# Index scores in pairs inside three input strips, the search from later strips on, and the layers written out

## What is computed

```python
dots = jnp.einsum('bthd,bsd->bths', qi.astype(jnp.float32), ki_all.astype(jnp.float32))
score = jnp.einsum('bth,bths->bts', wi.astype(jnp.float32), jax.nn.relu(dots))
allowed = (k_pos[None, :] // CHUNK) <= (q_pos[:, None] // CHUNK)
score = jnp.where(allowed[None], score, -jnp.inf)
top_val, top_idx = lax.top_k(score, topk)
...
logits = jnp.einsum('btngd,btknd->btngk', qg, kg).astype(jnp.float32) * (HEAD_DIM ** -0.5)
logits = jnp.where(valid[:, :, None, None, :], logits, -jnp.inf)
p = jax.nn.softmax(logits, axis=-1).astype(vg.dtype)
o = jnp.einsum('btngk,btknd->btngd', p, vg)
```

## Time and profile before

| | us |
|---|---|
| median of three runs (3303.45 to 3306.64) | 3303.59 |
| the profiled execution | 3304.65 |
| its span, first to last instruction | 3302.9 |
| layer 1: index scores between strips K and V | 175.05 to 226.60 |
| layer 1: end of the last count behind AU1 | 407.5 |
| change of layer, PE's first matmul of layer 2's norm | 1693.9 |

### The profile page before, as it was taken

The page is one execution under the profiler, slowest core; times in us unless marked ns, Lnnn a source line. Parts: engine busy times, 40 slices in busy tenths (PEclk is TensorE's granted clock), DMA queues, the critical chain, the costliest instruction groups (busy, mean ns, idle before and its releaser), DMA issues.

```text
span 3302.9 us, 44102 instructions
## 1 busy us (share of the span) xinstructions
PE 2926.2 (89%) x15746; PEld 2505.2 (76%) x15770; DVE 1611.5 (49%) x2488; ACT 1147.8 (35%) x1378; POOL 817.7 (25%) x340
## 2 busy tenths in 40 slices
PE   6699866788899999999979996678898999999996
PEld 6659732237799999999965993223688999999996
DVE  7658667653333232433455776666324414333244
ACT  1335737843321111111142483685324111111113
POOL 0101126711122222222210111763021222322221
PEclk9969978998899999999986997899899999999998
DMA  8202300010122222222211121001012222222222
GB/s 348 83 18 70 128 2 1 1 32 21 51 76 81 65 91 69 83 76 70 77 57 33 55 92 58 0 1 32 13 57 69 79 67 82 66 90 72 67 86 81
DMA packets 70265, 214.71 MB, mean 65 GB/s; under 512 B 17280, under 2 KB 17536, under 8 KB 69120
## 3 DMA queue, kind: packets, MB, share of 16 engines
q1 hardware_dynamic: 67504, 202.71, 18.2%
q10 hardware_dynamic: 2640, 10.49, 0.8%
HBM read 196.76 MB, written 15.87 MB: 64 GB/s over the span
## 4 chain that ended last, share of the span: by engine, by line
issue 50%; PE 30%; POOL 12%; DVE 4%; ACT 2%; DVEq 1%; POOLq 0%; ACTq 0%; DMA 0%
PE ps L823 26%; POOL cy L527 6%; POOL w_lo L501 6%; PE ps L998 1%; PE ps L982 1%; PE ps L1068 1%; ACT notsel L622 0%; PE ps L1047 0%; DVE smax L1424 0%; POOL hp L520 0%; DVE notsel L1305 0%; DVE s_keep L1257 0%; DVE notsel L1302 0%; DVE rank_samp L1297 0%; DVE negmax L1436 0%
## 5 line engine op out<-in xcount | busy, mean ns | idle before, releaser
L501 POOL TENSOR_TENSOR w_lo<-w_raw,w_hi 128x1024 fp32r<-128x1024 f32 x202 | 501.1, 2481 | 2207.4 <-ACT w_hi L582 2207.4
L823 PE MATMUL ps<-h_hi,w_hi 128*128 128x352 f32 x2928 | 646.6, 329 | 64.4 <-DVE h_lo L1126 50.1
L823 PE MATMUL ps<-h_hi,w_lo 128*128 128x352 f32 x2928 | 636.3, 325 | 0.0
L823 PE MATMUL ps<-h_lo,w_hi 128*128 128x352 f32 x2928 | 636.1, 326 | 0.0
L823 PEld LDWEIGHTS ps<-h_hi,w_hi 128*128 128x128 f32 x2928 | 502.8, 191 | 88.3 <-DVE h_lo L1126 61.5
L823 PEld LDWEIGHTS ps<-h_hi,w_lo 128*128 128x128 f32 x2928 | 507.0, 189 | 0.0
L823 PEld LDWEIGHTS ps<-h_lo,w_hi 128*128 128x128 f32 x2928 | 502.8, 190 | 0.0
L582 ACT CAST w_hi<-w_raw 128x1024 fp32r<-128x1024 f32 x202 | 211.2, 1045 | 643.3 <-PE ps L823 404.1
L527 POOL TENSOR_TENSOR cy<-cy,ctmp 128x1086 f32<-128x1086 f32 x120 | 302.3, 2520 | 234.2 <-ACT ctmp L708 224.4
L622 ACT ACTIVATE notsel<-score,s_cand 128x384 bf16<-128x384 f32 (+3 forms) x248 | 297.3, 1200 | 139.2 <-DVE s_cand L1245 139.0
L1528 DVE TENSOR_TENSOR act_f<-silu,ps 128x1056 f32<-128x1056 f32 x44 | 55.2, 1254 | 593.7 <-PE ps L823 593.7
(11 more groups left out here) (222 smaller groups left out, 3389.1 us busy)
## 6 DMA issues: line engine op xcount, KB each, us to landing
w_ada<-in_w_ada SPq DMA_DIRECT2D x96, 512.0 KB, 5.1
w_raw<-in_w_up SPq DMA_DIRECT2D x88, 512.0 KB, 3.4
w_raw<-in_w_in SPq DMA_DIRECT2D x34, 512.0 KB, 3.6
w_ada<-in_w_ada SPq DMA_DIRECT2D x7, 2048.0 KB, 12.2
w_raw<-in_w_down SPq DMA_DIRECT2D x32, 384.0 KB, 3.1
w_ada<-in_w_ada ACTq DMA_DIRECT2D x5, 2048.0 KB, 12.2
w_raw<-in_w_down SPq DMA_DIRECT2D x32, 320.0 KB, 2.9
spill<-stage SPq DMA_DIRECT2D x16, 528.0 KB, 2.6
```

The lines of the kernel that those rows point to most:

```text
L501: nc.gpsimd.tensor_tensor(w_lo[slot][:], w_raw[:], w_hi[slot][:].bitcast(F32), ALU.subtract)\
L823: last = nc.tensor.matmul(ps[:, bank + t, 0:TW], wt[slot][:, kk, :], mv[:, kk, t * TW:(t + 1) * TW], start=(kk == 0 and p == 0), stop=(kk ...
```

## The change

Three things change, and one follows from them.

1. The index scores are computed two heads at a time: heads 2hp and 2hp + 1 lie in the two halves of the partitions, and their contractions go to banks 6 and 7 together. There are 20 pairs in place of 40 steps; a pair has one ReLU over both banks on ACT and two operations on DVE. The pairs no longer stand between strips K and V. They are issued by `beside` behind the contraction blocks 0 to 6 of strips V, Q0 and Q1 (`PAIRS_IN`: 7, 7 and 6). All pairs use the same two banks, so a pair waits for the ReLU of the pair before. The two ReLU buffers are now the two buffers `probs` of the attention.
2. The search starts behind Q1's score pairs; `SEARCH_AFTER` gives one step behind Q1, two behind Q2 and Q3, three behind CA0 to AV1 and AU0, five behind AU1. The sample's index chunks move from V and later to Q2 and later (`SAMPLE_AFTER`), with SP's loads of their keys.
3. On every engine the loop over layers is a Python loop: the program contains both layers, and the values to wait for are constants, except in the inner loops that stay.

What follows: the copy of the sample's queries (`q_samp`) moves from Q3 to CG1, and ACT's copy of CA0 no longer waits for the sample's sums.

```diff
+PAIRS_IN = {4: (0, 7), 5: (7, 14), 6: (14, 20)}
+PAIR_AFTER = (0, 1, 2, 3, 4, 5, 6)
...
-SEARCH_AFTER = {S_V: 2, S_Q0: 2, S_Q1: 2, S_Q2: 2, S_Q3: 2, S_CA0: 3, S_CA1: 3, S_CG0: 3, S_CG1: 3, S_AV0: 3,S_AV1: 3, S_AU0: 2, S_AU1: 1}
+SEARCH_AFTER = {S_Q1: 1, S_Q2: 2, S_Q3: 2, S_CA0: 3, S_CA1: 3, S_CG0: 3, S_CG1: 3, S_AV0: 3, S_AV1: 3, S_AU0: 3, S_AU1: 5}
+SAMPLE_AFTER = S_Q2
...
+        relu = probs
...
-            with pe.Fori(0, DEPTH) as l:
+            for l in range(DEPTH):
                 rms(l, 0)
+
+                def dots(n):
+
+                    _, i, c, w, hp = DOTS[n]
+                    if n >= 1:
+                        pe.wait_ge(relu_ready.sem, relu_ready.at(l, n))
+                    for e in range(2):
+                        r = slice(64 * e, 64 * e + 64)
+                        last = nc.tensor.matmul(ps[:, 6 + e, 0:w], qi[r, hp, i * P:(i + 1) * P], ki[r, c:c + w], start=True, stop=True)
+                    last.then_inc(dots_ready.sem, 1)
...
-                    if j == S_K:
-                        for n in range(N_DOTS):
-                            relu_step(n, 6 + n % 2, DOTS[n][3])
-                    if S_V <= j < S_V + 5:
-                        c = j - S_V
+                    for n in range(*PAIRS_IN.get(j + 1, (0, 0))):
+                        relu_step(n, 2, DOTS[n][3])
+                    if SAMPLE_AFTER <= j < SAMPLE_AFTER + 5:
+                        c = j - SAMPLE_AFTER
...
-                    if j == S_K:
-                        for n, (sn, i, c, w, h) in enumerate(DOTS):
-                            sc = score[:, SC_AT[sn] + c:SC_AT[sn] + c + w]
-                            dve.wait_ge(relu_ready.sem, relu_ready.at(l, n + 1))
+                    for n in range(*PAIRS_IN.get(j + 1, (0, 0))):
+                        sn, i, c, w, hp = DOTS[n]
+                        sc = score[:, SC_AT[sn] + c:SC_AT[sn] + c + w]
+                        dve.wait_ge(relu_ready.sem, relu_ready.at(l, n + 1))
+                        for e in range(2):
+                            h = 2 * hp + e
...
+                    if j == S_Q0:
                         for sn, i in enumerate(SEARCHED):
...
-                    if j == S_K:
-
                         dve.drain()
                         start_search(0, PSRCH)
```

More of the change, by code:

```diff
@@ L168, in build @@
         swapped = place("swapped", Z_O, [P, TOK], F32)
-        relu = [place(f"relu{s}", Z_O + CYB + s * 2048, [P, 512], F32) for s in range(2)]
         wiT = place("wiT", Z_O + CYB, [P, TOK], F32)
@@ L497, in _ @@
         def _(pool):
-            with pool.Fori(0, DEPTH) as l:
+            for l in range(DEPTH):
                 def split_lo(j, slot):
@@ L604, in _ @@
                     nc.scalar.activation(cond_row[:], cond_row[:], ACT.Silu).then_inc(row_ready.sem, 1)
-            with act.Fori(0, DEPTH) as l:
+            for l in range(DEPTH):
                 act.wait_ge(x_fed.sem, x_fed.at(l, 0))
@@ L813, in rms, with strip @@
                 last.then_inc(rms_summed.sem, 1)
-            def strip(l, j, slot, bank, nk, hi, lo, k_ready=None):
+            def strip(l, j, slot, bank, nk, hi, lo, k_ready=None, beside=None):
                 pe.wait_ge(w_ready.sem, w_ready.at(l, j + 1))
@@ L825, in strip @@
                                                     start=(kk == 0 and p == 0), stop=(kk == nk - 1 and p == 2))
-                last.then_inc(w_used.sem, 1)
+                    if kk == nk - 1:
+                        last.then_inc(w_used.sem, 1)
+                    if beside is not None:
+                        beside(kk)
             pe.wait_ge(const_loaded.sem, 32)
@@ L849, in _, with dots_beside @@
                         pe.wait_ge(wi_rows.sem, wi_rows.at(l, 1))
-                    strip(l, j, j % 2, strip_bank(j), KD, h_hi, h_lo, (h_ready, 0) if j == 0 else None)
+                    if j == S_V:
+                        pe.wait_ge(idx_rot.sem, idx_rot.at(l, 3))
+                        pe.wait_ge(ki_twice.sem, ki_twice.at(l, 16))
+                        pe.wait_ge(wi_ready.sem, wi_ready.at(l, 1))
+                    def dots_beside(kk):
+                        first, end = PAIRS_IN[j]
+                        if kk in PAIR_AFTER and first + PAIR_AFTER.index(kk) < end:
+                            dots(first + PAIR_AFTER.index(kk))
+                    strip(l, j, j % 2, strip_bank(j), KD, h_hi, h_lo, (h_ready, 0) if j == 0 else None,
+                          dots_beside if j in PAIRS_IN else None)
                     if j == S_QI1:
@@ L1200, in _ @@
             swap_pairs = [i ^ 1 for i in range(32)]
-            with dve.Fori(0, DEPTH) as l:
+            for l in range(DEPTH):
                 norm(l, 0)
```

56 lines of the change are left out of this document (23 added, 33 removed).

## The result

The changed kernel takes 3274.11 us, the median of four runs (3271.37 to 3275.21), and the kernel before took 3304.36 beside it: a ratio of 0.9906, with a 95% interval of 0.9889 to 0.9923. It is 30 us faster. The forecast was 3274, from 3258 to 3290.

The account below looks back on a forecast made before the run. Bound: PE up to the last score, then the DVE and ACT search chain to the counts' end. Gains 2 x 12.8 + 3.2 + 1 = 29.8 us off 3304.65 give 3274.9, less 1.06 for the median: 3274, range 3258 to 3290.

Parts of the forecast that it names:

- What bounds the stage: Scores and search: PE spends 53.6 us a layer on scores and aftermath, then DVE and ACT set the pace until the counts end.
- The pairs: Twenty score pairs in strips V, Q0 and Q1: 14.1 us of columns plus 4.0 fixed, 18.1; with three strips 53.2.
- the sum by its rule: Total if each of the twenty score pairs pays twice for switching the tiling mode: 3276.
- The waits between pairs: Each pair waits for the previous ReLU: about 0.4 us left for two handovers, just enough; Q1's third ReLU 1.1 us late.
- The search: Last score to end of counts on DVE and ACT: 165.4 us instead of 179.0; counts end 12.8 us earlier per layer.
- The layer change: Between the two layers: writing them out removes the jump back, saving 3.2 us, once.
- Constants: Wait values in both layers become constants instead of computed registers: 1 us gained in all, bounds 0 and 10.
- A: Rival, score pairs: handover too tight, each pair waits half a microsecond for its ReLU, 10 us a layer; 3294, chance 0.08.
- B: Rival, score stage: PE is the bound after all, so 34.4 us a layer come through; 3231, chance 0.07.
- C: Rival, score pairs among strips: PE falls to the lower clock, adding 49.2 us a layer; 3372, chance 0.04.
- D: Rival, behind the counts: they end earlier but the next stage starts no earlier; 3299, chance 0.03.

## Why the prediction was right, point by point

**What bounds the stage.** Right. I had read 53.6 us a layer of PE's time in the stage and its aftermath; AU1's last matmul comes 31.6 us earlier against K's rotation, and only 12 of these reach the end of the counts. Moving steps from late to early strips changed nothing, lengthening the pairs on PE by 14.4 us a layer cost all of it, and hiding one step paid its 4.0. So PE is last up to the last score, the chain of DVE and ACT from there on. The wait of 2 to 3 us that I expected of PE before CA1 is not there; between the weave and AU1's end PE never waits longer than 0.2 us.

**The pairs.** This step was mis-sized. I took 0.2 us beside the columns, from the attention's pair, and a bound of 0.05 more from the earlier trace rows. It is 0.40, so twenty pairs take 21.9 us and not 18.1. The rows that I used held it: in the earlier trace rows the strip's first group behind the sample's contraction (241.35) takes 0.75 us where a group in the stream takes 0.65, and I left that 0.1 out; with it and the issue ahead, those rows give 1.2 for a pair and not 1.1. Whether the attention's pair hides the same 0.1 in the matmuls behind it, its rows do not separate. The Trainium skill (TensorEngine Tiling (Array Packing), Key Properties) says that switching the tiling mode drains TensorE; the run with each pair twice agrees, 0.40 us for a pair that enters and leaves the shape and nothing for one that stays in it, though the shape is not all that changes there. The page has no figure; the sum by its rule, 3276, had used mine. My range had 4 us over both layers for dearer pairs, and they were dearer by 7.6.

**The waits between pairs.** The handover of 0.4 us was enough, with 0.2 more that the switches gave. The microsecond that I put on the third pair in Q1 did not come: a ReLU of Q1 did wait 2.2 us for DVE, but the longer slots left PE just behind it. The last score stands 56.6 us behind K's rotation; by my sum it was 54.1.

**The search.** Start 9.6 for 9.7; Q1's rotation 5.1 for 5.9; Q3's stretch, to CA0's copy, 12.9 for 13.8; CA0 to AU0 78.4 for 77.6; AU1's copy to the end 28.8 for 28.8. From the last score to the end 163.7 for 165.4. Two errors of opposite sign, +2.5 and -1.7, leave 12.0 us in layer 1 for the 12.8 predicted, 12.6 in layer 2. That they nearly cancel is luck.

**The layer change.** 3.4 for 3.2; the hand is 0.1 us. **Constants.** I took 1 us over both layers. In the stage of the edit that is right (the ends of the counts are the same with loops and without, 220.3). In the total it is not: with its loops back the kernel is 18 us slower, of which the jump is 3.4, and the 14 left are above my bound of 10 too. I had written 3278 for it and measured 3291.84. The forecast of the whole came out because the changed kernel's attention and strips took about what they took before; had they taken what the kernel with loops takes, it would have been some 14 us slower and at the edge of the range. And the profiled span holds 3.2 us behind layer 1's counts that I had not forecast, against 2.1 lost at its start and end. That the total lies within 0.2 us of the forecast is luck. A term for the clock's return behind each wait was missing: the attention takes 322.5 to 325.9 us a layer in the profiles with written-out layers and up to 329.2 in those with loops.

**The rivals.** A: no pair waits. B: refuted by the run with early steps, and by the 9.4 us that PE stands idle for AU1's copy ahead of the centring (369.29). C: the clock never left 1.00 in the weave; in the block of pairs it fell behind a wait of 3.19 us at the fourth pair and stayed at the lower level while PE waited up to 1.2 us for each ReLU. The Trainium skill (TensorE: Matmul & The Clock Gate, A second HAM failure mode: psum-queue depth-cycling) describes, of a bf16 kernel, a clock that goes back and forth between its levels when PE idles shortly between groups of matmuls. The weave has no such idles and kept the upper level; the block has them, but its clock stayed at 0.50 and did not go back and forth. D: the stage behind the counts started earlier by as much as they ended earlier, and a little more (the attention's first `probs` 51.1 us behind them, not 52.6).

## What to carry to other kernels

Time freed on one engine is worth only what reaches the chain that ends last: before moving work, find that chain and count how much of the freed time reaches it. In this kernel small matmuls that depend on other engines cost little between the matmuls of a large one (0.40 us a pair beside their columns, no wait, clock 1.00); in a block of their own they waited 1.2 us each, at a clock of 0.50. When two edits are made at once, undo each alone before the gain is divided between them: here the written-out layers alone gave 11 us, the rest alone 13, and together 30.

## What the runs showed of the hardware

- Going from full-array fp32r matmuls to 64-row f32 contractions and back cost 0.40 us each time on PE, with one pair or two in it: a pair of 512 columns adds 1.25 us, a second one behind it 0.87.
- Behind the same wait, PE's granted clock comes back at different times. After 4.06 us of idle, one or two pairs of 512 columns ran at the lower level (2.08 us each, 1.13 at full clock); after 8.06 us three to six strip groups ran at 0.88 us instead of 0.485. A layer's attention differs by up to 7 us between kernels whose work there is the same, and by 0 to 3.4 between the two layers of one execution; how much of that is the clock is not shown.
- The jump back of the layer loop cost 3.4 us between DVE's last product and PE's release, in the kernel before and in the one with its loops back. The Trainium skill (Runtime: NRT & Kernel Launch, Instruction fetch mechanics) says that a taken branch to a page not yet fetched stalls; the rows agree with that, and no run here shows that the fetch is what takes the time.
- With written-out layers a chain of forty handovers between three engines was 1.3 us shorter, 0.03 us each, and not shorter where the handovers lie under other work. Whether the constants to wait for do this or the straight code is not shown.
- A DVE operation on 1056 columns (L1229 in the two kernels with the closer pairs) took 3.29 us when a split of POOL of 2.5 us overlapped it, four times of four, and 1.26 the 24 times without.
